# Half-size products for the gate projection beside the first gated scan, router logits by column groups, and the joins and running sums of the scan at other steps

## What is computed

```python
def _chunk_gated_scan(q, k, v, log_g):          # chunks of 32 tokens
    b = jnp.cumsum(log_g, axis=2)
    ref = b[:, :, CHUNK // 2 - 1:CHUNK // 2]
    s = einsum('bnthk,bnshk->bnhts', q * jnp.exp(b - ref), k * jnp.exp(ref - b))
    ...
def _mixer_ab(h, w_in, gate_up, gate_bias, norm_gain, w_out, rel_bias):
    proj = jnp.einsum('bsd,df->bsf', h, w_in)
    qa, ka, va, qb, kb, vb, lr_f, lr_b, gate = _split(proj, ...)   # gate: 1536 columns
    oa = dilated_attention(heads(qa, 8), heads(ka, 8), heads(va, 8), rel_bias)
    g_f = jax.nn.log_sigmoid(lr_f @ up[0] + gb_[0]) / 16
    g_b = jax.nn.log_sigmoid(lr_b @ up[1] + gb_[1]) / 16
    ob = bidirectional_gated_scan(qh, kh, heads(g_f, 4), kh, heads(g_b, 4), heads(vb, 4))
    y = jnp.concatenate([oa, _head_rmsnorm(ob, norm_gain)], axis=-1) * jax.nn.silu(gate)
    return jnp.einsum('bsf,fd->bsd', y, w_out)
```

```python
x = x + m_lat[2] * mix_lat
h_lat = modulate(rms_norm(x, norm2_g), m_lat[3], m_lat[4])
aff = jax.nn.softmax(jnp.einsum('btd,de->bte', h, router_w), axis=-1)
gate, idx = lax.top_k(jnp.swapaxes(aff, 1, 2), cap)      # 128 tokens for each expert
```

## Time and profile before

| | |
|---|---|
| time, median of 3 | 3872.6 us (3872.45 to 3874.2) |
| profiled execution | 3873.76 us, of which its span is 3872.0 |
| stage gla, first to last instruction | 660.2 to 969.2 us |
| stage mix, to the first read of all logits | 3256.0 to 3426.2 us |
| PE busy over the span | 3474.3 us (90%) |
| mean granted PE clock | 0.944 |

### The profile page before, as it was taken

How to read it: one execution, slowest core, us unless ns; L and a number is a source line. 1 busy time by engine, 2 the same in 40 slices (tenths; PEclk the granted TensorE clock), 3 DMA queues, 4 the chain that set the end, 5 groups by cost and what they waited for, 6 DMA issues and landing times. The chain is left out here.

```text
span 3872.0 us, 47862 instructions
## 1 busy us (share of the span) xinstructions
PE 3474.3 (90%) x16721; PEld 2277.8 (59%) x16721; DVE 1949.0 (50%) x4104; ACT 1088.4 (28%) x2201; POOL 1242.9 (32%) x982
## 2 busy tenths in 40 slices
PE   8999998999698999999988798999977877939997
PEld 3745776778344676676656445565566875524443
DVE  2036663543683376667687453335489586240002
ACT  1024333442341233334343352222113112111112
POOL 2120101343343356556556363002302544311111
PEclk9999998999898999999999898999988878969999
DMA  4264543231632121221211634123425713346998
GB/s 135 77 180 139 166 125 100 86 107 55 229 153 63 50 58 54 63 58 47 58 52 45 257 141 109 42 64 106 144 65 167 267 52 130 121 179 238 317 319 292
DMA packets 417636, 494.59 MB, mean 128 GB/s; under 512 B 71058, under 2 KB 321194, under 8 KB 417411
## 3 DMA queue, kind: packets, MB, share of 16 engines
q1 hardware_dynamic: 390695, 463.64, 36.2%
q0 software_dynamic: 4752, 17.30, 1.7%
q10 hardware_dynamic: 21964, 10.75, 1.0%
HBM read 362.85 MB, written 128.77 MB: 127 GB/s over the span
## 5 line engine op out<-in xcount | busy, mean ns | idle before, releaser
L1091 POOL TENSOR_TENSOR hgrn_queries<-hgrn_qd,hgrn_pair_decay 128x640 f32<-128x640 f32 x192 | 263.0, 1389 | 294.4 <-PE hgrn_ps_a L1206 253.5
L1141 PE MATMUL hgrn_ps_w<-xT,hgrn_ring 128*128 128x512 f32 x432 | 196.5, 601 | 1.8 <-PEq L34 1.8
L415 PE MATMUL gla_bg_ps<-gla_bg_w,xT 128*128 128x256 f32 x768 | 186.1, 387 | 0.0
L554 POOL TENSOR_TENSOR l_wsum<-l_ring 128x512 f32<-128x512 f32 x14 | 20.0, 1431 | 508.0 <-PE att_bg_ps L586 187.2
L1757 PE MATMUL end_ps_z<-end_w,end_yT 128*128 128x512 f32 x384 | 166.9, 594 | 1.4 <-ACT end_yT L1700 1.4
L2927 PE MATMUL end_ps_z<-end_w,end_yT 128*128 128x512 f32 x384 | 166.8, 594 | 1.5 <-ACT end_yT L2847 1.5
L415 PEld LDWEIGHTS gla_bg_ps<-gla_bg_w,xT 128*128 128x128 f32 x768 | 145.7, 194 | 26.0 <-issue 6.8
L1311 DVE TENSOR_TENSOR hgrn_k_end<-hgrn_kd,hgrn_end_decay 128x128 f32<-128x128 f32 x168 | 137.1, 855 | 9.2 <-issue 2.6
L1141 PEld LDWEIGHTS hgrn_ps_w<-xT,hgrn_ring 128*128 128x128 f32 x432 | 81.8, 194 | 94.4 <-issue 94.2
L2205 ACT ACTIVATE att_s_sb<-att_s_sb,att_shift 128x256 f32<-128x256 f32 (+1 forms) x192 | 88.9, 464 | 166.3 <-DVE att_shift L2162 166.3
L1141 PE MATMUL hgrn_ps_w<-hgrn_xs,hgrn_wsum 128*128 128x512 f32 x288 | 130.9, 602 | 4.2 <-ACT hgrn_sig L1425 4.2
(11 more groups left out here) (711 smaller groups left out, 7824.0 us busy)
## 6 DMA issues: line engine op xcount, KB each, us to landing
expw_wg<-in_exp_w_gate_dram SPq DMA_DIRECT2D x16, 2048.0 KB, 10.8
expw_wu<-in_exp_w_up_dram SPq DMA_DIRECT2D x16, 2048.0 KB, 16.3
expw_wd<-in_exp_w_down_dram SPq DMA_DIRECT2D x16, 2048.0 KB, 21.9
att_w_ada<-in_ada_w_dram SPq DMA_DIRECT2D x24, 1024.0 KB, 6.5
hgrn_ring<-in_w_in_c_dram SPq DMA_DIRECT2D x18, 1024.0 KB, 5.5
l_ring<-in_w_in_ab_dram SPq DMA_DIRECT2D x14, 1024.0 KB, 5.6
end_gt<-gate_l SPq DMA_DIRECT2D x16, 768.0 KB, 8.4
hgrn_ring<-in_w_in_c_dram SPq DMA_DIRECT2D x24, 512.0 KB, 5.3
```

The lines of the kernel that those rows point to most:

```text
L415: last = pe.matmul(bank[0:job.rows, q * job.width:(q + 1) * job.width], job.acts[:, k, t * P:t * P + job.rows], w[:, k, 0:job.width], star ...
L1091: pool.tensor_tensor(queries[:, d, s, :].rearrange("p (b a c) -> p b a c", b=POINTS, a=PC), q, f, ALU.mult).then_inc(queries_done, 1)
L1141: last = pe.matmul(bank[:, :], a[:, k, :], x(k), start=(fresh and k == 0), stop=(k == HK - 1), skip_group_check=True)
```

## The change

Stage gla: the Background job is replaced by Halves on 6 units (`gates` in the network code), with the first two weight units loaded during attention into two of the three ring buffers, which are now separate tensors. The half sums stay in xT (L2576 is gone). LEAD is 8 fills, the slots are 95. POOL makes the weight sums of unit 0 before its constants, the others behind the queries of a later step. DVE gets `bg.join` at three places of a step. The bias of the gates is loaded in the attention stage. The decay inputs are made one matmul a call, into one bank: two calls in step 0 and two in step 1; for head 0 all four into four banks, behind the first product. `sums` is split: L2482 and the scan at steps 2 and 4, the relative values with `spans_of` at steps 3 and 5 (`relative`); `grown` for both directions at step 6; `exps` at steps 4 and 6. z and grow share a tensor, so do mag and rel.

Stage mix: the router weights, padded to 32 columns, are the stationary side and the turned h moves: 8 matmuls of 128 columns, each into one of four 32-row groups of a bank (`by_group`), ACT copies the bank (`move_groups`), one matmul with a selection matrix adds the four groups (`logits`). For tile 7 the two additions of POOL are done by DVE.

```diff
@@ class Halves
+        self.RING, self.coming = len(ring), list(units) + list(following)
@@ def low_rank_scan
-    LEAD = 4
+    LEAD = 8
+        ps_z = pbank("ps_z")
+        first_z = (ps_z, ps_k, ps_u, ps_o)
-        bg = Background(sb, sem, pbank, jobs, 3 * STEPS, 3, 2, 3, lead=LEAD)
+        bg = Halves(sem, xT, xs, ring, wsum, bg_stage, [pbank(f"bg_ps{b}") for b in range(3)], units, 3 * STEPS - 1, 2, lead=LEAD)
+        def sums_after(u):
+            return max(1, (bg.ended_in[7 * u - 1] - LEAD) // 3 + 2)
@@ gpsimd
+            bg.sums(pool, 0)
             make_identity(pool, ident)
...
                     scale_queries(h, p)
-                    if h + 1 < heads and p in (5, 6):
-                        scale_keys_in(h + 1, p - 5)
+                    if TILES * h + p in sums_due:
+                        bg.sums(pool, sums_due[TILES * h + p])
+                    if h + 1 < heads and p in (6, 7):
+                        scale_keys_in(h + 1, p - 6)
@@ tensor
+            def gates(h, i):
+                d, half = i // 2, i % 2
+                rows = rank_rows(d)
+                if h:
+                    pe.wait_ge(z_moved, 4 * h + i)
+                pe.matmul((ps_z if h else first_z[i])[:, :], ups[rows, h * P:(h + 1) * P], low[rows, half * BANK:(half + 1) * BANK],
+                          start=True, stop=True).then_inc(z_made, 1)
@@ vector
-            low_rows = slice(0, KB // 2)
-            dve.tensor_tensor(xT[:, low_rows, BANK:SEQ], xT[:, low_rows, BANK:SEQ], xT[:, low_rows, 0:BANK], ALU.add).then_inc(restored, 1)
...
                 pick(h, p)
+                bg.join(dve, LEAD + 3 * g)
                 if p < CARRIED:
                     carry_on(h, p)
+                bg.join(dve, LEAD + 3 * g + 1)
                 if p + 1 < CARRIED:
                     scale_keys(h, p + 1)
                 if h + 1 < heads:
                     prepare(h + 1, p)
                 if p == CARRIED and h + 1 < heads:
                     scale_keys(h + 1, 0)
+                bg.join(dve, LEAD + 3 * g + 2)
@@ def mix_and_route, tensor
-            def logits(t):
+            def by_group(t):
                 pe.wait_ge(h_moved, 2 * t + 2)
...
+                wait(pe, q_moved, t)
                 for k in range(KB):
-                    last = pe.matmul(ps_l[:, t * E:(t + 1) * E], hT[:, t % 2, k, :], rw[:, k, :], start=(k == 0), stop=(k == KB - 1))
-                last.then_inc(l_made, 1)
+                    rows = slice(GROUP * (k % GROUPS), GROUP * (k % GROUPS + 1))
+                    last = pe.matmul(ps_q[rows, t % 2 * P:(t % 2 + 1) * P], rw[:, k, :], hT[:, t % 2, k, :],
+                                     start=(k < GROUPS), stop=(k >= KB - GROUPS), skip_group_check=True)
+                last.then_inc(q_made, 1)
+
+            def logits(t):
+                pe.wait_ge(q_moved, t + 1)
+                pe.matmul(ps_l[:, t * E:(t + 1) * E], quarters[:, :], sel[:, :], start=True, stop=True).then_inc(l_made, 1)
@@ scalar
+            def move_groups(t):
+                act.wait_ge(q_made, t + 1)
+                wait(act, l_made, t)
+                act.activation(quarters[:, :], ps_q[:, t % 2 * P:(t % 2 + 1) * P], ACT.Copy).then_inc(q_moved, 1)
@@ vector
+                if t == LAST:
+                    dve.drain()
+                    dve.tensor_tensor(part[:, t % 2, :], part[:, t % 2, :], xt[:, t % 2, :], ALU.add).then_inc(summed, 1)
```

More of the change, by code:

```diff
@@ L467, in __init__ @@
         self.slots, self.lead = lead + slots, lead
-        self.loads_by = [16 * sum(1 for v in range(held, u + 1) if v % self.RING == u % self.RING) for u in range(len(units))]
+        self.loads_by = [16 * sum(1 for v in range(held, u + 1) if v % self.RING == u % self.RING) for u in range(len(self.coming))]
         total = sum(self.count(f) * self.columns(f) for f in range(lead, len(self.fills)))
@@ L508, in load @@
     def load(self, sp, u):
-        unit = self.units[u]
+        unit = self.coming[u]
         if u >= self.RING:
@@ L517, in fetch @@
             u, i = self.fills[f]
-            if end == g - 1 and i == LAST and u + self.RING < len(self.units):
+            if end == g - 1 and i == LAST and u + self.RING < len(self.coming):
                 self.load(sp, u + self.RING)
@@ L547, in end @@
             sp.wait_ge(self.stored[n], 16 * (1 + n // 2) * len(self.units))
+        for u in range(len(self.units), len(self.coming)):
+            sp.wait_ge(self.w_loaded[u % self.RING], self.loads_by[u])
     def sums(self, pool, u):
@@ L2055, in _ @@
             load_ada(1)
+            with nc.allow_non_contiguous_dma(reason="a bias for each partition"):
+                for d in range(2):
+                    sp.dma_start(gate_shift[:, d, :], gate_bias[d].rearrange("(c p) -> p c", p=P)).then_inc(shift_loaded, 16)
             for g in range(HEADS * ST):
@@ L2386, in _ @@
                     scale_queries(h, p)
-                    if h + 1 < heads and p in (5, 6):
-                        scale_keys_in(h + 1, p - 5)
+                    if TILES * h + p in sums_due:
+                        bg.sums(pool, sums_due[TILES * h + p])
+                    if h + 1 < heads and p in (6, 7):
+                        scale_keys_in(h + 1, p - 6)
         @block.tensor
         def _(pe):
-            def gates(h, half):
-                wait(pe, z_moved, 4 * h + 2 * half)
-                for d in range(2):
-                    rows = rank_rows(d)
-                    last = pe.matmul(ps_z[d][:, :], ups[rows, h * P:(h + 1) * P], low[rows, half * BANK:(half + 1) * BANK], start=True, stop=True)
-                last.then_inc(z_made, 1)
+            def gates(h, i):
[5 more added lines that the diff above has]
+                          start=True, stop=True).then_inc(z_made, 1)
             def front(g):
@@ L2448, in output @@
                 last.then_inc(out_done, 1)
-            pe.wait_ge(low_loaded, 96)
-            for half in range(2):
-                gates(0, half)
-            pe.wait_ge(restored, 1)
-            for n in range(LEAD + 1):
+            bg.multiply(pe, 0)
+            pe.wait_ge(low_loaded, 64)
+            for i in range(4):
+                gates(0, i)
+            for n in range(1, LEAD + 1):
                 bg.multiply(pe, n)
@@ L2637, in _ @@
                 act.dma_start(ups[rank_rows(d), :], up[d]).then_inc(low_loaded, 16)
-                with nc.allow_non_contiguous_dma(reason="a bias for each partition"):
-                    act.dma_start(shift[:, d, :], gate_bias[d].rearrange("(c p) -> p c", p=P)).then_inc(low_loaded, 16)
-            act.wait_ge(low_loaded, 96)
-            gates(0, 0)
-            gates(0, 1)
-            for d in range(2):
-                logs(0, d)
-                bg.move(act, 2 * d)
-                bg.move(act, 2 * d + 1)
+            for i in range(4):
+                gates(0, i)
+            for n in range(2):
+                bg.move(act, n)
+            logs(0, 0)
+            bg.move(act, 2)
+            bg.move(act, 3)
+            logs(0, 1)
+            bg.move(act, 4)
             exps(0, 0)
@@ L2650, in _ @@
             decays(0, 1)
+            for n in range(5, LEAD):
+                bg.move(act, n)
             for g in range(STEPS):
@@ L4839, in _ @@
             branch.pad(pool)
+            pool.memset(rw[:, :, :], 0.0).then_inc(rw_clear, 1)
+            pool.memset(sel[:, :], 0.0)
+            pool.drain()
+            for n in range(GROUPS):
+                rows = slice(GROUP * n, GROUP * n + E)
+                pool.tensor_copy(sel[rows, :], ident[rows, rows])
+                pool.drain()
             pool.memset(halves[:, :, :], 0.0)
@@ L4849, in finish_h @@
                 pool.tensor_tensor(out[:, t % 2, :], scaled[:, :], shift[:, :], ALU.add).then_inc(h_done, 1)
-            for t in range(TILES):
+            for t in range(LAST):
                 pool.wait_ge(gated, t + 1)
@@ L4992, in scale @@
                                          op0=ALU.mult, op1=ALU.mult).then_inc(scaled_done, 1)
+                if t == LAST:
+                    wait(dve, h_turned, 2 * (t - 1))
+                    wait(dve, h_stored[b], 16 * (t // 2))
+                    dve.drain()
+                    dve.tensor_tensor(out[:, b, :], scaled[:, :], shift[:, :], ALU.add).then_inc(h_done, 1)
             for t in range(TILES):
```

155 lines of the change are left out of this document (92 added, 63 removed).

## The result

The changed kernel takes 3854.6 us (median; 3849.3 to 3858.8) beside 3874.2 for the kernel before: 19.6 us less by the medians. The ratio of the two is 0.9945 (95% interval 0.9934 to 0.9956), which is 21 us. A later comparison gave 0.9951 (0.9937 to 0.9965). I had forecast 3835.4 with a range of 3825 to 3851: the sign is right, but the gain is little over half of the 37 us, and the time lies outside the range.

A forecast was written before the change was run, and what follows sets the result against it. PE was taken to set the pace from about 724 us on. The terms, -16.2 + 6.0 - 11.8 - 4.8 - 3.8 + 0.5 - 7.1, gave -37.2 us, a median of 3835.4, range 3825 to 3851.

The forecast's parts named there:

- Term 1: Products of the scan stage: 1344 records of 128 columns at 0.1117 us replace 768 of 256 columns, -16.2 us.
- Rival (b): Scan products do not pay: half-size records cost 0.138 us as in attention, so 3871 us, no change; chance 0.04.
- estimate of 0.162 us a record: Scan products counted as two passes a record: 217.7 us in all, +51.4 instead of -16.2; counted within a chance of 0.04.
- Term 2: Decay inputs in steps 0 and 1 of three heads: single-matmul calls of 1.13 us, +6.0 us (+2.9 to +7.5).
- Term 3: Start of the scan stage gla: first front near 699, -11.8 us (bounds -7 and -13).
- Term 4: First step of the scan: PE's clock stays after a wait under 2 us, -4.8 us (0 to -5.3).
- Term 5: Stalls of the three scan heads, 7.6 us: half of them go, -3.8 us (-7.6 to +3).
- The move of the output: End of the scan stage: the move now comes last and costs two stores, +0.5 us.
- Term 6: Router stage: logits by 32-column groups and a shorter tail, -7.1 us (-4 to -9).
- a sign for the tail: Router stage: 5.5 to 6 us less from the last `mix` matmul's end to the first logits read.
- Rival (a): Waits stay in the scan: start gives 9 us, stalls remain, decay inputs cost their upper bound; -22 us, 3850; chance 0.20.
- Rival (c): Slower: scan products reusing a bank wait for DVE's joins, 34 at 1.5 us each, 51 us more, 3886; chance 0.03.

The follow-up runs named there:

- the last version: Changed kernel with POOL's sums and key scaling in four pieces, finished products moved ahead of logs and exponentials, last tile's square sum first: 3838.5 us, later 3839.0.
- the router alone: The kernel before, with its old scan stage and only the router stage changed: 3867.9 us, 0.9987 of before.

## Why the forecast was wrong, point by point

**Term 1, the products: right.** 0.112 us a record in the steps, ordinary steps of 7.17 to 7.18 (7.2 forecast). Rival (b) is out. So is the estimate of 0.162 us a record that I had worked out from the Trainium skill ("TensorE: Matmul & The Clock Gate", section "Back-to-back issue gap"). Only where a product begins or ends in the middle of a step is it 7.40 to 7.49, about 1 us in all that I had not counted. (The rows that I read give 0.2163 and 0.1119 us a record, not 0.2165 and 0.1117; that makes the term -15.7 instead of -16.2.)

**Term 2, the decay inputs: right mechanism, its upper bound.** A step with two calls takes 9.67 for 7.18, 1.25 us a call, so single matmuls cost as much as the overlapping pairs did: +7.4 us instead of +6.0.

**Term 3, the start: right.** First front at 698.07 (699 forecast); 38.0 us from the start of the stage, of which the products are 29.8, so the term was -12.8 for -11.8.

**Term 4: right, by a little more.** Step 0 took 8.49 us, beside 8.82 and 9.03 in heads 1 and 2, so the term was -5.6 for -4.8. The clock is not lost there: the granted clock was 1.00 from 698 to 718.

**Term 5, the stalls: wrong, and this is the step that failed.** I kept half of 7.6 us, a gain of 3.8, with +3 as the worst. The long steps (12.90, 9.07, 11.74, 8.00 and 13.74 for 7.18) are 19.6 us, so the term was +12.0. Heads 1 and 2 took 66.1 and 67.5 us, where I had 60 to 61.5 and the kernel before 64.7. I had the facts in hand: I counted the 20 POOL sums, and I wrote that an operation of DVE beside POOL takes up to 2.28 us for 1.23. The trace of the kernel before even had a small one, 1.27 us for 0.21 beside POOL's queries, in each of the first three heads (least, median, most in ns):

```profile
L2493 DVE TENSOR_TENSOR gla_to_mid<-gla_cum x8: 205/207/1273, 685.2 to 889.8; 128x32 f32<-128x32 f32 x8
```

But I put them into a budget of busy time (6.4 of 7.2 us in a heavy step), with the stretching as a factor on the long operations. What counts is that it is not a factor: each two-input operation waits for the rest of POOL's, so an operation of 0.2 us costs up to 1.3 and one of 0.32 up to 2.5. `gla_to_mid` and the spans are five such small operations almost in a row. Where they stand in step 6 of head 0, the change put 6.4 us of POOL's sums (744.79 to 751.19), with pauses of only 0.16 us. In the step of 13.74 us the harm is indirect: the sums came just before and made POOL late, so that its queries and key scaling stood beside the spans. The runs without the sums (13.3 us back) and with them in pieces (7.2 back) show it. Most of the rest came from POOL's key scaling (6.6 back), which was there before and met the spans only now. The two figures with pieces add up to 13.8 us. They are not separate shares of the 19.6, since each cut also moves the steps in which DVE meets POOL. Of the 19.6 us, 1.9 us is another cause, ACT's logs ahead of the move of a product in step 3 of head 0, which the last version removed.

The clock also belongs here. I had looked for its loss only at the first front. It is lost behind each of the three long waits, and adds 1.9 to 3.0 us a time; these are part of the 19.6.

**The move of the output:** the next stage begins 23.7 us behind the last matmul, 22.8 before: +0.9 for +0.5.

**The sum of the scan stretch.** The rest of term 1 -16.6, the step edges +1.2, the decay inputs +7.4, the first step -5.6, the stalls +12.0 and the move +0.9 make -0.7, and the trace has -0.5. So no large term is missing.

**Term 6, the router: right in total.** 7.1 us. A tile gives 0.89 instead of 0.76, and the square sum of the last tile was late by 0.88 instead of 0.65. The sixteen group records took 0.58 us for 0.55, and the joining matmul 0.24 with its switch of the array, so the switches cost less than the 0.1 each that I had taken. Up to the last `mix` matmul the stage gave 4.2 us (4.1 forecast) and in the tail 2.9 (3.05 by the terms). The 5.5 to 6 us that I had named as a sign for the tail did not fit my own terms and did not come.

**The unchanged stages.** The profile of the changed kernel has 3.8 us more there. The layer behind the second closing stage took 240.7 us instead of 238.1; the clearest difference is the granted clock in one of its stretches, before and after:

```profile
2218.30:2238.30 20.00, 16.03 (x52) 7.93 (x51) 12.04 (x25) 12.28 (x37) 11.16 (x4) 1.00 0.33 138
```

```profile
2206.00:2226.00 20.00, 16.04 (x48) 7.74 (x48) 11.95 (x26) 12.28 (x37) 10.71 (x4) 0.91 0.36 148
```

PE is as busy in both. In all eleven executions with the changed scan this layer takes 240.6 to 243.3 us, and 238.1 in both with the old one, the router alone among them. So some 2.6 us of the gain are given back there, at a lower granted clock. What in the scan sets this 1300 us later was not tried and stays open. Over all unchanged stages the executions scatter more (2283.0 to 2292.5 around the 2286.0 of before), so only the 2.6 us of this layer repeat, not the whole 3.8.

**The rivals.** Rival (a), the waits stay, at 3850, had the right direction and was nearest to the measured time, but partly by luck, since it put the loss in other places: it let the start and the decay inputs slip and kept the stalls, while the start was as forecast and the stalls grew. Rival (c) named POOL stretching DVE, but looked for the wait at the banks; PE waited for DVE's join once, 3.1 us in the start, and never in a step. The range was too narrow since the bound of term 5 held one small new wait a head and not the lock of two engines.

## What to carry to other kernels

Work that is put on an idle POOL is not free for DVE: list which of DVE's operations with two SBUF inputs stand beside it, and price each at the rest of the POOL operation, however small it is itself. Where it can't be moved, cut POOL's long operations into pieces, those that stood there before as well as the new ones (272.7 us with the sums in four, 266.1 with the key scaling too), and keep chains of small DVE operations away from it. A budget of busy time cannot show this; the timelines of both engines in one step do.

## What the runs showed of the hardware beside this

- A piece of a POOL operation costs 0.45 us at 128x128 and 0.72 at 128x256, against 1.27 for 128x512. So four quarters hold POOL for 1.8 us at least instead of 1.27, and the scan stretch was still 7.2 us shorter.
- A matmul of 16 rows and 512 columns alone on the array costs 1.25 us in the middle of other work, as much as two that overlap.
- A `copy` of 128x8 on DVE takes 0.16 to 0.17 us alone and is held up by POOL as well: 0.47 us beside pieces of 128x128, 0.74 beside pieces of 128x256, and 1.28 beside whole queries (five times in four of the runs). Before and after the change it took 0.17 in every place, but there it never began inside a POOL operation except in its last few hundredths of a us. It reads one tensor only, so I had taken it for safe. The rule quoted above makes an exception for two-port modes; whether this copy ran in one, no trace shows. One of the five, with key scaling in pieces:

```profile
813.42 1.28 DVE L2533 COPY gla_ends<-gla_totals 128x8 f32<-128x8 f32 x1
```
